# Seven block products for 18 of the 22 gate/up tile pairs of a streaming-encoder layer

## The reference, cut to what matters

```
x = x + rmsnorm(m @ W_out) * g_post_mix
h = rmsnorm(x) * g_pre_ffn
g, u = split(h @ w_gate_up)                    # h is 512 x 1024, w_gate_up 1024 x 5632
x = x + rmsnorm((silu(g) * u) @ w_down) * g_post_ffn
```

## Time and profile before

| | |
|---|---|
| runs (3) | 778.24, 778.35, 778.73 us; median 778.35 |
| profiled execution, first to last instruction | 777.0 us |
| the same execution's own time | not listed apart from the runs; their median is 1.35 us above the span |
| TensorE busy | 770.5 us, 99% |
| VectorE, ScalarE, GpSimd busy | 377.3, 347.1 and 414.1 us |
| mean granted TensorE clock | 0.998 of full speed |

### The profile page before, as it was taken

The page is one execution under the profiler, slowest core; times in us unless marked ns, Lnnn a source line. Parts: engine busy times, 40 slices in busy tenths (PEclk is TensorE's granted clock), DMA queues, the critical chain, the costliest instruction groups (busy, mean ns, idle before and its releaser), DMA issues.

```text
span 777.0 us, 10403 instructions
## 1 busy us (share of the span) xinstructions
PE 770.5 (99%) x3665; PEld 646.0 (83%) x3665; DVE 377.3 (49%) x536; ACT 347.1 (45%) x555; POOL 414.1 (53%) x253
## 2 busy tenths in 40 slices
PE   9999999999999999999999999999999999999997
PEld 7788888888888888888889888888888888888885
DVE  4979989986566664399055100000000011444564
ACT  5762287777677766441364222122221222223243
POOL 6936366866688696234640344444434444443462
PEclk9999999999999999999999999999999999999999
DMA  9653441231224223135641133233322333223312
GB/s 336 175 155 101 143 122 55 61 103 54 62 62 118 66 61 110 55 89 183 215 136 55 55 108 90 73 107 108 108 74 88 108 108 107 65 98 108 108 54 109
DMA packets 102441, 81.50 MB, mean 105 GB/s; under 512 B 3200, under 2 KB 91272, under 8 KB 102408
## 3 DMA queue, kind: packets, MB, share of 16 engines
q1 hardware_dynamic: 102216, 81.06, 33.5%
q10 hardware_dynamic: 192, 0.01, 0.0%
HBM read 76.85 MB, written 3.68 MB: 104 GB/s over the span
## 4 chain that ended last, share of the span: by engine, by line
PE 97%; issue 1%; DMA 0%; POOL 0%; DVE 0%; ACT 0%; POOLq 0%; SPq 0%
PE ps L507 25%; PE ps L486 20%; PE ps L488 20%; PE ps L487 20%; PE ps L573 3%; PE ps L731 2%; PE ps L720 2%; PE ps L703 1%; PE ps L705 1%; PE ps L626 1%; PE ps L625 1%; PE ps L551 0%; DMA wq_raw<-in_first 0%; POOL x L1396 0%; PE ps L604 0%
## 5 line engine op out<-in xcount | busy, mean ns | idle before, releaser
L1219 POOL TENSOR_TENSOR w_lo<-raw,w_hi 128x1024 fp32r<-128x1024 f32 x74 | 177.1, 2395 | 237.1 <-ACT w_hi L842 218.6
L486 PE MATMUL ps<-h_hi,w_hi 128*128 128x512 f32 (+1 forms) x608 | 235.6, 388 | 0.0
L488 PE MATMUL ps<-h_hi,w_lo 128*128 128x512 f32 (+1 forms) x608 | 233.8, 385 | 0.0
L487 PE MATMUL ps<-h_lo,w_hi 128*128 128x512 f32 (+1 forms) x608 | 233.7, 384 | 0.0
L842 ACT ACTIVATE w_hi<-raw 128x1024 fp32r<-128x1024 f32 (+1 forms) x70 | 74.3, 1061 | 271.3 <-PE ps L488 195.4
L488 PEld LDWEIGHTS ps<-h_hi,w_lo 128*128 128x128 f32 x608 | 114.2, 188 | 22.5
L487 PEld LDWEIGHTS ps<-h_lo,w_hi 128*128 128x128 f32 x608 | 114.4, 188 | 21.1
L486 PEld LDWEIGHTS ps<-h_hi,w_hi 128*128 128x128 f32 x608 | 114.3, 188 | 21.1
L1723 DVE TENSOR_TENSOR act<-silu,ps 128x512 f32 (+1 forms) x22 | 15.1, 688 | 211.3 <-PE ps L488 211.3
L1335 POOL TENSOR_TENSOR w_lo<-raw,w_hi 128x1024 fp32r<-128x1024 f32 x30 | 78.3, 2613 | 30.4 <-ACT w_hi L990 30.1
L1728 DVE TENSOR_TENSOR d_lo<-act,d_hi 128x512 fp32r<-128x512 f32 x18 | 43.1, 2396 | 51.7 <-ACT d_hi L1152 51.7
(11 more groups left out here) (228 smaller groups left out, 1321.2 us busy)
## 6 DMA issues: line engine op xcount, KB each, us to landing
raw<-in_w_gate_up SPq DMA_DIRECT2D x44, 512.0 KB, 4.3
raw<-in_w_in SPq DMA_DIRECT2D x40, 512.0 KB, 4.4
raw<-in_w_down SPq DMA_DIRECT2D x22, 512.0 KB, 3.9
raw<-in_w_out SPq DMA_DIRECT2D x8, 512.0 KB, 4.3
x_t<-in_first SPq DMA_DIRECT2D x8, 256.0 KB, 6.9
wq_raw<-in_first SPq DMA_DIRECT2D x8, 256.0 KB, 6.4
x_in<-in_x SPq DMA_DIRECT2D x4, 512.0 KB, 7.5
qi_twice<-qi_hi SPq DMA_DIRECT2D x16, 128.0 KB, 2.3
```

What stands on the lines that cost most here:

```text
L486: mm(acc, whi_c, a_hi_, start=first, stop=False)
L487: mm(acc, whi_c, a_lo_, start=False, stop=False)
L488: return mm(acc, wlo_c, a_hi_, start=False, stop=last)
L1219: nc.gpsimd.tensor_tensor(w_lo[:, at(u), :], raw[:, at((d % 2) * 2 + u), :], w_hi[:, at(u), :], sub).then_inc(w_lo_done, 1)
```

## The change

Pairs 4 to 21 (18 pairs, `p` = 0 to 17) are no longer computed tile by tile. A pair is a 2x2x2 block product: {gate, up} x {first, second half of the 1024 contraction rows} x {first, second 256 tokens}. It takes eight block products; the change uses seven, in the manner of Strassen and Winograd. With G0, G1, U0, U1 the quarters of the pair's weights (4 chunks each) and X(k, t) the quarters of h:

- four sums of weight quarters per pair: U1+U0, G0+U0, (U1+U0)+G0, and that plus G1 (VectorE, `sum_of`);
- four sums of the quarters of h, made once (`t_sums`: GpSimd makes `early` = hi + lo of the first token half, ScalarE copies a part of the second from PSUM as `late`, VectorE makes the four, ScalarE and VectorE split them);
- seven products of 12 matmuls of 128x256 (`product`, `seven`), in three banks `m`, `gate` and `c`. The first (G0·X) starts `m`; ScalarE copies `m` into `gate` (`first_kept`), and the chain of products in `gate` goes on from that copy; `m` itself goes on as well. ScalarE also keeps `c` after the second product (`fifth_kept`) and `m` after the third (`sixth_kept`). VectorE adds what was kept (`up_2`, `gate_two`), ScalarE makes the two silu halves, and VectorE multiplies (`finish_pair`).

Of a pair's seven weight parts (three quarters, four sums), ScalarE makes all high halves (`quarters_hi`, `sums_hi`), VectorE six low halves in three instructions (`quarters_rest`, `sums_rest`), and GpSimd the seventh (`last_quarter`), where it made both low halves of 128x1024 before. While TensorE works on pair p, ScalarE and VectorE run `window(p)`: they prepare pair p+1 and take in pair p. Two sets of banks (4 to 6 and 0 to 2) and two sets of weight parts alternate. The up tile of a pair is loaded in two DMAs, with its halves exchanged.

Pairs 0 to 3 stay as they were (pairs 2 and 3 outside of a loop), as do the w_down tiles, whose halves now lie in `wn_hi` and `wn_lo`; their first tile takes the token blocks in the order 2, 3, 0, 1. Some buffers lie elsewhere, and a few semaphores near the start of the program are merged (`warm_eps_set`, `r_done`, `small_kept`). The core of the diff (empty lines are left out):

```diff
-        for j in range(2):
+        for j in range(PLAIN):
...
-        with sp.Fori(2, FC) as j:
-            pair(j + T_UP // 2, j, cols(wup, 0, P, FF))
-        loop(T_DOWN, FC // 2, rows(w_down[0]))
+        def quarters(p, v):
+            gate, up_ = (raw[:, 2 * v + u, :].rearrange("p (c n) -> p c n", c=KC) for u in range(2))
+            sp.dma_start(gate, wup[:, :, at(p * P + PLAIN * P, P)]).then_inc(up_in, 16)
+            for k in range(2):
+                half = slice(KC // 2 * (1 - k), KC // 2 * (2 - k))
+                sp.dma_start(up_[:, KC // 2 * k:KC // 2 * k + KC // 2, :],
+                             wup[:, half, at(p * P + (PLAIN * P + FF), P)]).then_inc(up_in, 16)
+        def raw_free(n):
+            sp.wait_ge(sum_made, n * 4)
+            sp.wait_ge(parts_lo_done, n * 3)
+            sp.wait_ge(last_lo_done, n)
...
+        for p in range(2, SEVENS):
+            sp.wait_ge(up_in, p * 48)
+            raw_free(p - 1)
+            quarters(p, p % 2)
...
-        with pe.Fori(1, FC // 2) as j:
-            up(j)
+        up(1)
+        def product(acc, hi, lo, first_col, b_hi, b_lo, first):
+            for c in range(KC // 2):
+                col = slice(first_col + c * P, first_col + (c + 1) * P)
+                mm(acc, hi[:, col], b_hi[:, c, :], start=first and c == 0, stop=False, skip_group_check=True)
+                mm(acc, hi[:, col], b_lo[:, c, :], start=False, stop=False, skip_group_check=True)
+                ins = mm(acc, lo[:, col], b_hi[:, c, :], start=False, stop=c == KC // 2 - 1, skip_group_check=True)
+            return ins
...
+        def seven(p, v):
+            first_bank = 4 - 4 * v
+            m, gate, c = (bank(first_bank + n, HALF) for n in range(3))
+            q_hi_, q_lo_, s_hi_, s_lo_ = quart_hi[v], quart_lo[v], sum_hi[v], sum_lo[v]
+            pe.wait_ge(parts_hi_done, p * 3 + 1)
+            pe.wait_ge(parts_lo_done, p * 3 + 1)
+            pe.wait_ge(act_done, p + (1 + PLAIN))
+            product(m, q_hi_, q_lo_, 0, *h_quarter(0, 0), True).then_inc(product_done, 1)
+            pe.wait_ge(parts_hi_done, p * 3 + 2)
+            pe.wait_ge(parts_lo_done, p * 3 + 2)
+            pe.wait_ge(summed_up, p * 2 + 2)
+            product(c, s_hi_, s_lo_, 0, *t_sum(0), True).then_inc(product_done, 1)
+            pe.wait_ge(product_kept, p * 3 + 1)
+            product(m, s_hi_, s_lo_, Q, *t_sum(2), False).then_inc(product_done, 1)
+            product(gate, q_hi_, q_lo_, Q, *h_quarter(1, 0), False).then_inc(product_done, 1)
+            pe.wait_ge(parts_hi_done, p * 3 + 3)
+            pe.wait_ge(parts_lo_done, p * 3 + 3)
+            pe.wait_ge(product_kept, p * 3 + 3)
+            product(m, s_hi_, s_lo_, 2 * Q, *t_sum(1), False).then_inc(product_done, 1)
+            product(c, s_hi_, s_lo_, 3 * Q, *h_quarter(1, 1), False).then_inc(product_done, 1)
+            pe.wait_ge(last_lo_done, p + 1)
+            pe.wait_ge(summed_up, p * 2 + 5)
+            product(m, q_hi_, q_lo_, 2 * Q, *t_sum(3), False).then_inc(product_done, 1)
...
+        mm(bank(5, HALF), h_hi[:, 0, 0:P], h_hi[:, 0, 0:HALF], start=True, stop=True).then_inc(product_done, 1)
+        seven(0, 0)
+        pe.wait_ge(act_done, 2 + PLAIN)
+        with pe.Fori(0, SEVENS // 2 - 1) as j:
+            for v in (1, 0):
+                seven(j * 2 + (2 - v), v)
+        seven(SEVENS - 1, 1)
...
+        sc.wait_ge(h_lo_done, TB)
+        run(late[:, :, :].rearrange("p c (t n) -> p c t n", n=P), halves_of(0), ACT.Copy).then_inc(t_hi_done, 1)
...
+        for n in range(2):
+            sc.wait_ge(t_done, 2 * n + 2)
+            for i in (2 * n, 2 * n + 1):
+                run(t_hi[:, i, :, :], t_sums[:, i, :, :], ACT.Copy).then_inc(t_hi_done, 1)
+        def quarters_hi(p, v):
+            sc.wait_ge(up_in, p * 48 + 48)
+            run(quart_hi[v][:, 0:2 * Q], raw[:, 2 * v, :], ACT.Copy)
+            run(quart_hi[v][:, 2 * Q:3 * Q], raw[:, 2 * v + 1, 0:Q], ACT.Copy).then_inc(parts_hi_done, 1)
+        def sums_hi(p, v, n):
+            sc.wait_ge(sum_made, p * 4 + (n + 3))
+            part = slice(2 * Q * n, 2 * Q * (n + 1))
+            run(sum_hi[v][:, part], sums[v][:, part], ACT.Copy).then_inc(parts_hi_done, 1)
...
+        def first_kept(p, v):
+            sc.wait_ge(product_done, p * 7 + 2)
+            run(bank(5 - 4 * v, HALF), bank(4 - 4 * v, HALF), ACT.Copy).then_inc(product_kept, 1)
+        def fifth_kept(p, v):
+            sc.wait_ge(product_done, p * 7 + 3)
+            sc.wait_ge(summed_up, p * 2 + 3)
+            run(p5_kept[:, :], bank(6 - 4 * v, HALF), ACT.Copy).then_inc(product_kept, 1)
+        def sixth_kept(p, v):
+            sc.wait_ge(product_done, p * 7 + 4)
+            sc.wait_ge(summed_up, p * 2 + 4)
+            run(u2[:, :], bank(4 - 4 * v, HALF), ACT.Copy).then_inc(product_kept, 1)
+        def silu_gates(p, v):
+            sc.wait_ge(product_done, p * 7 + 5)
+            sc.wait_ge(act_done, p + (2 + PLAIN))
+            run(silu[:, 0, 0:HALF], bank(5 - 4 * v, HALF), ACT.Silu).then_inc(silu_done, 1)
+            sc.wait_ge(summed_up, p * 2 + 6)
+            run(silu[:, 0, HALF:S], gate_2[:, :], ACT.Silu).then_inc(silu_done, 1)
+        def window(p, v):
+            quarters_hi(p + 1, 1 - v)
+            first_kept(p, v)
+            sums_hi(p + 1, 1 - v, 0)
+            fifth_kept(p, v)
+            sixth_kept(p, v)
+            sums_hi(p + 1, 1 - v, 1)
+            silu_gates(p, v)
...
+                sc.wait_ge(product_done, j * 14 + (7 * (2 - v) + 1))
+                window(j * 2 + (2 - v), v)
...
+        sc.wait_ge(product_done, 7 * p + 1)
+        split(T_DOWN // 2, 0, wn_hi)
+        first_kept(p, 1)
+        split(T_DOWN // 2, 1, wn_hi)
+        fifth_kept(p, 1)
+        sixth_kept(p, 1)
         round_act(0, 0)
         round_act(1, 1)
-        up(FC // 2 - 1)
+        silu_gates(p, 1)
...
-        with gp.Fori(T_UP // 2 + 2, (T_END - LAST) // 2) as d:
+        gp.wait_ge(x_normed, TB)
+        for k in range(2):
+            part = slice(KC // 2 * k, KC // 2 * (k + 1))
+            nc.gpsimd.tensor_tensor(early[:, part, :], h_hi[:, part, 0:HALF], h_lo[:, part, 0:HALF],
+                                    ALU.add).then_inc(early_made, 1)
+        for d in range(T_UP // 2 + 2, T_DOWN // 2):
             for u in range(2):
                 split(d, u)
+        def last_quarter(p, v):
+            gp.wait_ge(parts_hi_done, p * 3 + 1)
+            part = slice(2 * Q, 3 * Q)
+            nc.gpsimd.tensor_tensor(quart_lo[v][:, part], raw[:, 2 * v + 1, 0:Q], quart_hi[v][:, part],
+                                    sub).then_inc(last_lo_done, 1)
+        with gp.Fori(0, SEVENS // 2) as j:
+            for v in range(2):
+                last_quarter(j * 2 + v, v)
+        with gp.Fori(T_DOWN // 2, (T_END - LAST) // 2) as d:
+            for u in range(2):
+                split(d, u, wn_hi, wn_lo)
...
+        late_down = ps[:, 5:8:2, :].rearrange("p t (c n) -> p c t n", n=P)
+        tt(t_plain(0), early[:, 0:KC // 2, :], late[:, :, :], sub).then_inc(t_done, 1)
+        tt(in_blocks(t_plain(1)), late_down, in_blocks(late[:, :, :]), sub).then_inc(t_done, 1)
+        ve.wait_ge(t_done, 1)
+        for t in range(2):
+            col = slice(t * P, (t + 1) * P)
+            ins = stt(t_plain(2)[:, :, col], t_plain(0)[:, :, col], -1.0, late_down[:, :, t, :], ALU.mult, sub)
+        ins.then_inc(t_done, 1)
+        ve.wait_ge(t_done, 3)
+        stt(t_plain(3), t_plain(2), -1.0, early[:, KC // 2:KC, :], ALU.mult, sub).then_inc(t_done, 1)
+        up(0)
+        def t_rest(i):
+            ve.wait_ge(t_hi_done, i + 2)
+            ve.wait_ge(t_done, 4)
+            tt(t_lo[:, i, :, :], t_plain(i), t_hi[:, i, :, :], sub).then_inc(t_done, 1)
...
+        def sum_of(p, v, i, x_, y_, made=None):
+            if made:
+                ve.wait_ge(sum_made, p * 4 + made)
+            tt(sums[v][:, i * Q:(i + 1) * Q], x_, y_, ALU.add).then_inc(sum_made, 1)
...
+        def first_sums(p, v):
+            ve.wait_ge(up_in, p * 48 + 48)
+            sum_of(p, v, 0, quarter(v, 3), quarter(v, 2))
+            sum_of(p, v, 2, quarter(v, 0), quarter(v, 3))
+        def second_sum(p, v):
+            sum_of(p, v, 1, sum_part(v, 0), quarter(v, 0), 1)
+        def third_sum(p, v):
+            sum_of(p, v, 3, sum_part(v, 1), quarter(v, 1), 3)
+        def quarters_rest(p, v):
+            ve.wait_ge(parts_hi_done, p * 3 + 1)
+            tt(quart_lo[v][:, 0:2 * Q], raw[:, 2 * v, :], quart_hi[v][:, 0:2 * Q], sub).then_inc(parts_lo_done, 1)
+        def sums_rest(p, v, n):
+            ve.wait_ge(sum_made, p * 4 + 4)
+            ve.wait_ge(parts_hi_done, p * 3 + (n + 2))
+            part = slice(2 * Q * n, 2 * Q * (n + 1))
+            tt(sum_lo[v][:, part], sums[v][:, part], sum_hi[v][:, part], sub).then_inc(parts_lo_done, 1)
+        def up_2(p, v):
+            ve.wait_ge(product_done, p * 7 + 6)
+            ve.wait_ge(product_kept, p * 3 + 2)
```

(34 more changed lines are left out.)

195 lines of the change are left out of this document (144 added, 51 removed).

## The result

The changed kernel takes **764.26 us** (median of 4 runs, 764.02 to 764.95), the kernel before 778.54 (median of 4, 778.24 to 778.90); the ratio is 0.9818, with a 95% interval from 0.9804 to 0.9832. The profiled execution took 764.12 us with a span of 762.2. Forecast were 764.2 us and a span of 762.7.

What follows compares the result with a forecast made beforehand. TensorE's matmuls were taken as the bound: 195.87 us removed, 181.44 plus 0.12 added, so span 777.0 - 14.3 = 762.7; 1.35 for runs over span and 0.2 for seam waits gave 764.2 us, range 763.6 to 770.0.

Steps and rivals of the forecast that it cites:

- TensorE's sum: First plain wide matmul to first w_down matmul: 217.63 us before, 203.32 after, 14.3 less if TensorE never waits.
- the seams: Entry to and exit from the seven-product pairs: preparation hidden with some 4 us to spare, 0.2 us added for small waits.
- GpSimd's hold: A two-SBUF-input VectorE instruction stands still during GpSimd's low half: 1.14 us more, once a pair.
- The good case: ScalarE rounds the first sums from 2.6 us into a pair; the copy of `m` ends at 4.97, 0.7 early.
- the worse case: The hold precedes the third sum: ScalarE rounds from 3.7 us, its copies end about 5.5, 0.2 early for the fifth product.
- Rival A: VectorE's and ScalarE's instructions don't overlap: fifth product 0.31 us late a pair, 5.6 in all, 769.8 us; chance 0.22.
- Rival B: Register instructions at loop waits cost 0.10 us each, on top of Rival A: 18.2 us in all, 782.4; chance 0.09.
- C: TensorE's own sequencer can't hide its register instructions and waits: 0.38 us a pair, 6.9 in all, 771.1; chance 0.05.
- D: Narrow matmuls at another pitch: 0.1295 us saves nothing, or 0.109 gives 747.6 us; chance 0.02 together.

Runs made afterwards that it cites:

- e9_chain: The changed kernel with each VectorE instruction of a window waiting by semaphore for the end of the one ahead; 778.05 us, ratio to before 0.9995.
- e2_plain12: The changed kernel with twelve tile pairs plain and ten by seven products, instead of four and eighteen; 771.04 us.
- e7_unrolled: The changed kernel with the loops over pairs written out on TensorE, ScalarE, VectorE and GpSimd, so waits stand against constants; 764.41 us.
- e5_pool_two: The changed kernel with GpSimd making a second low half (512 columns), taken from VectorE's work; 766.15 us.
- e4_vec_more: The changed kernel with one more VectorE subtraction of 1024 columns in each pair's window, written where nobody reads it; 775.10 us.
- e8_unrolled_vec_more: The changed kernel with the loops over pairs written out and one more VectorE subtraction of 1024 columns a window; 774.70 us.
- e11_scal_more: The changed kernel with one more ScalarE copy of 1024 columns a window, ahead of the copy the fifth product waits for; 771.77 us.

## Why the prediction was right, point by point

- **TensorE's sum.** 14.3 us forecast, 14.29 in the stage. The narrow pitch of 0.1200, read from 96 matmuls ahead of the stage, held for 1512. The figure of the Trainium skill that I had set aside ("TensorE: Matmul & The Clock Gate", Back-to-back issue gap), which the page gives for an isolated matmul, would have made it 109 ns.
- **The total.** The span was forecast 0.5 us too long. The program ahead of the stage ended 0.59 us earlier (433.62 for 434.21). In the thirteen profiles of the changed kernel and its variants, alike ahead of the stage, that point lies between 433.33 and 434.91, so this is scatter. The 0.2 us added for small waits at the seams weren't there either. Against that, a run's time lies 1.85 to 1.92 us above its own span, and not 1.35: I had taken the span of one run from the median of others. Two errors of half a microsecond cancel, so that the final number is right to 0.1 us is luck; what was right by its mechanism is the 14.3 us.
- **VectorE.** Forecast: `up_2` ends at 8.16, 0.3 to 0.4 us early with the handoff. Seen: 8.01 and 8.10, 0.54 and 0.63 early before a handoff of 0.05, so 0.5 to 0.6. The sum was near, and the slack a little underrated. GpSimd's hold was forecast at 1.14 and is 0.98; in its place the fourth sum starts 0.12 us later than an overlap would have let it, since it waits for the third; the low half itself takes 1.81 on GpSimd on average, not 1.29, which nobody waits for. VectorE is busy for 84% of a pair (134.83 of 161.40 us over 16 pairs), just under my 85 to 92%: in that line I took too little off for the overlaps.
- **ScalarE.** The good case: the sums are rounded from 2.68 (2.6 forecast), the copy of `m` ends at 4.98 (4.97 forecast). ScalarE's rounding starts as soon as the third sum is made, so it matters that GpSimd's hold falls on the fourth. I had left this open between 2.6 and 3.7. The turns decide it: the third sum starts before GpSimd's instruction or with it (538.12 and 538.11) and goes through; in e9_chain it starts 0.1 us later and is held. So the good case rests on about 0.1 us of timing that the prediction didn't work out, and here it had luck; the worse case would have cost nothing either, as e9_chain shows at the fifth product.
- **The seams.** The low halves of the sums of h ended at 439.1 (440 forecast), the first pair's parts at 452.8 (452), asked for at 455.5. So 2.7 us to spare where I said 4. e2_plain12 bounds what the seams cost at about 0.1 us, the size of the one matmul that opens the `gate` bank.
- **Rival A** had the wrong place. It charged 0.08 for an instruction and put the loss at the fifth product, 0.31 us a pair. e9_chain ties each instruction to the one ahead, and the fifth product isn't late, though GpSimd's hold lies where A had put it; the seventh is, by 0.79 us a pair with its new start. But e9_chain has more in it than A: each of its waits brings a handoff, 0.12 to 0.21 where A lost 0.08. What A alone would cost no run shows. An estimate from these rows: seven lost overlaps make 0.56, where 0.5 to 0.6 were to spare, so about 0.1 us a pair with the new start, some 766. A didn't come true because VectorE starts the next instruction early in this order too: `quart_lo` and `sum_lo` start 1.14 us apart at 1.21 us long.
- **Rival B** named 0.10 us for every instruction with a register wait. e7_unrolled shows 0.01 over the whole chain from the first sum to `up_2`, where the events are past, and from nothing to 0.23 at a wait that blocks. **C** and **D** cost nothing anywhere.

No version that makes all seven products and adds them up in full was faster than the change. TensorE has no gap left in the stage, so of this scheme only fewer plain pairs could help, 0.80 us each. The first pair's parts, ready at 452.8, would then be asked for at 444.6; that wasn't tried.

## What to carry to other kernels

Price a scheme that saves multiplications by the pitch of the matmul that it makes, not by its count: seven narrow products gave 7.4% of a pair where the count says 12.5%, eight would have lost 6%, and a further halving of the width would lose it all, since 128 columns take 0.112 us against 0.120 for 256. Then write the helpers' work of one pair on TensorE's clock and find the slack at each product that asks; here it was 0.5 us in 10, and tying VectorE's instructions to each other by waits ate all of the gain. Work moved from VectorE to GpSimd while both read two SBUF operands took more from VectorE than it gave: price it by the rest of GpSimd's instruction that is left when VectorE's next one is due, not by the work moved.

## What the runs showed of the hardware that I had not expected

- VectorE and GpSimd, each reading two SBUF operands, take turns by the order of their starts. A held VectorE sum of 512 columns ends 0.55 us behind GpSimd's end (0.545 to 0.553 in 17 pairs). A low half of 512 columns on GpSimd takes 1.29 us when it is first (e9_chain) and up to 1.86 when it has to wait for a sum. VectorE loses 0.98 us a pair, and 1.08 more in e5_pool_two.
- A matmul that comes late by 0.02 us costs 0.12: the second matmul behind a wait starts 0.22 us after the first instead of 0.12 (e4_vec_more, e5_pool_two). It is 0.19 where the handoff took 0.15 and not 0.05 (e8_unrolled_vec_more: 550.58 to 550.77 us; e11_scal_more, in a loop, the same).
- A wait of VectorE for its own instruction just ahead costs 0.12 to 0.21 us against none, in a loop (e9_chain).
- A wait that blocks against a register's value, in a loop, costs between nothing and 0.23 us more than against a constant (e7_unrolled: 0.27 and 0.03 from ScalarE's silu to VectorE); one whose event is past costs nothing that shows.
